# Row tiles issued by GpSimd in one written-out order with the modulation tiles; SyncE issues weight tiles only

## The reference

```python
def first_block(x, c, ...):                  # layers "layer0", "layer1"
    c_act = silu(c)
    for l in range(2):
        sh1, sc1, gt1, sh2, sc2, gt2 = split(c_act @ w_ada[l] + b_ada[l], 6)
        h = x * (1 + sc1) + sh1
        y = token_mixer(h, w_in[l], b_in[l], ...)   # differential, forgetting, retention branches
        x = layernorm(ALPHA * x + gt1 * y, ln_g[l, 0], ln_b[l, 0])
        h = x * (1 + sc2) + sh2
        y = conv_ffn(h, w_up[l], w_conv[l], b_conv[l], w_down[l])
        x = layernorm(ALPHA * x + gt2 * y, ln_g[l, 1], ln_b[l, 1])
    return x

def second_block(x, ...):                    # "middle", then the experts
    x = layernorm(ALPHA_2 * x + gated_deltanet(x, ...), ...)
    x = layernorm(ALPHA_2 * x + swiglu(x, ...), ...)
    x = layernorm(ALPHA_2 * x + swa_sink_attention(x, ...), ...)
    x = layernorm(ALPHA_2 * x + moe_swiglu(x, ...), ...)    # 8 experts, top 2
    return x
```

## Time and profile before

| | |
|---|---|
| median of 3 runs | 2850.41 us (2846.89 to 2853.26) |
| span of the profiled execution | 2847.6 us; its own time outside the profiler is not given |
| PE busy | 2629.9 us, 92% |
| DVE busy | 2177.1 us, 76% |
| ACT busy | 1516.4 us, 53% |
| POOL busy | 24.1 us, 1% |
| DMA | 671.68 MB, mean 236 GB/s |
| chain that ended last | PE 67%, DVE 21%, ACT 5%, issue 4%, DMA 3% |

### The profile page before, as it was taken

One profiled execution on the slowest core, in us unless ns is written; L12 is line 12 of the kernel. 1 busy time (PEld: TensorE's weight loads), 2 busy tenths in 40 slices (PEclk: granted clock), 3 DMA queues, 4 the chain that ended last, 5 costly groups with the idle time before them and its releaser, 6 DMA issues.

```text
span 2847.6 us, 36585 instructions
## 1 busy us (share of the span) xinstructions
PE 2629.9 (92%) x13986; PEld 2234.2 (78%) x13986; DVE 2177.1 (76%) x2738; ACT 1516.4 (53%) x1786; POOL 24.1 (1%) x46
## 2 busy tenths in 40 slices
PE   7889889998998889979989988899999999999997
PEld 6667669876777779868979966788888888888885
DVE  6777677778766777666766556798988989898896
ACT  2344445433344345436334344577777777777774
POOL 0000000000000000000000000000000000000000
PEclk9999999999999999989999999799999999999998
DMA  9743436576544455443125582499999999999994
GB/s 359 273 155 133 143 127 245 200 275 255 213 150 133 144 193 203 163 151 113 45 74 189 173 249 78 189 363 349 370 343 370 343 351 364 347 370 344 368 347 177
DMA packets 104754, 671.68 MB, mean 236 GB/s; under 512 B 11984, under 2 KB 12240, under 8 KB 27136
## 3 DMA queue, kind: packets, MB, share of 16 engines
q1 hardware_dynamic: 97584, 622.08, 59.0%
q0 software_dynamic: 6992, 47.19, 4.9%
HBM read 665.03 MB, written 4.19 MB: 235 GB/s over the span
## 4 chain that ended last, share of the span: by engine, by line
PE 67%; DVE 21%; ACT 5%; issue 4%; DMA 3%; PEld 0%; DVEq 0%; SPq 0%; ACTq 0%; PEldq 0%
PE bank L852 20%; PE bank L854 19%; PE bank L853 19%; DVE W_low L2263 7%; PE bank L1287 3%; ACT W_high L1740 2%; DVE work L2348 1%; DVE arena L2253 1%; DMA arena<-in_w_layer 1%; PE bank L1620 1%; DMA W<-in_w_layer 1%; DMA W<-in_w_middle 1%; DVE work L2580 1%; PE bank L935 1%; DVE acted L2563 1%
## 5 line engine op out<-in xcount | busy, mean ns | idle before, releaser
L2263 DVE TENSOR_TENSOR W_low<-W,W_high 128x1024 fp32r<-128x1024 f32 x426 | 496.7, 1207 | 287.9 <-ACT W_high L1740 282.0
L1740 ACT ACTIVATE W_high<-W 128x1024 fp32r<-128x1024 f32 x426 | 421.8, 1039 | 406.6 <-PE bank L854 186.6
L853 PE MATMUL bank<-W_low,arena_parts 128*128 128x512 f32 (+1 forms) x1128 | 444.8, 394 | 0.0
L852 PE MATMUL bank<-W_high,arena_parts 128*128 128x512 f32 (+1 forms) x984 | 396.5, 403 | 24.3 <-DVE W_low L2263 14.0
L854 PE MATMUL bank<-W_high,arena_parts 128*128 128x512 f32 (+1 forms) x984 | 388.4, 395 | 0.0
L854 PE MATMUL bank<-hT_high,W_low 128*128 128x256 f32 (+2 forms) x1208 | 347.9, 288 | 0.0
L852 PE MATMUL bank<-hT_high,W_high 128*128 128x256 f32 (+1 forms) x1088 | 316.5, 291 | 28.2 <-DVE W_low L2263 20.0
L853 PE MATMUL bank<-hT_low,W_high 128*128 128x256 f32 (+1 forms) x1088 | 311.4, 286 | 0.0
L852 PE MATMUL bank<-W_high,hT_high 128*128 128x512 f32 (+1 forms) x640 | 264.2, 413 | 25.3 <-DVE W_low L2263 11.0
L852 PE MATMUL bank<-arena_parts 128*128 128x512 f32 x672 | 269.4, 401 | 1.5 <-issue 1.5
L853 PE MATMUL bank<-W_low,hT_high 128*128 128x512 f32 (+1 forms) x672 | 266.7, 397 | 0.0
(11 more groups left out here) (428 smaller groups left out, 4791.7 us busy)
## 6 DMA issues: line engine op xcount, KB each, us to landing
W<-in_w_layer SPq DMA_DIRECT2D x170, 1024.0 KB, 4.9
W<-in_w_expert SPq DMA_DIRECT2D x148, 1024.0 KB, 5.1
arena<-in_w_expert SPq DMA_DIRECT2D x114, 1024.0 KB, 4.9
W<-in_w_middle SPq DMA_DIRECT2D x58, 1024.0 KB, 4.9
arena<-in_w_layer POOLq DMA_DIRECT2D x40, 1024.0 KB, 7.3
consts<-in_w_expert SPq DMA_DIRECT2D x37, 1024.0 KB, 4.9
R<-in_w_expert SPq DMA_DIRECT2D x37, 1024.0 KB, 4.9
R<-in_rows_layer SPq DMA_DIRECT2D x70, 256.0 KB, 5.8
```

Of the source, the lines that this page charges most:

```text
L852: mm(bank, lhs[0], rhs[0], start=start, stop=False)
L853: mm(bank, lhs[0], rhs[1], start=False, stop=False)
L1740: do(high_slot(at, w)[:, cols], raw(at, w)[:, cols], ACT.Copy).then_inc(main_highs.filled[main_highs.slot(at, w)], 1)
L2263: tt(lows(at, w)[:, cols], raw(at, w)[:, cols], high_slot(at, w)[:, cols].bitcast(F32), ALU.subtract).then_inc(*low_ready.event(at))
```

## The change

SP's program keeps the weight tiles of the layers and the middle, and loses all 97 row tiles of these parts and the four of the end. POOL's program gets them. For the two layers a list written out by hand, `POOL_LOADS`, puts the row tiles and the modulation tiles into one order; the order within each kind stays as it was. For the middle POOL issues the first eleven row tiles, the two transfers of the bias table with the wait between them, and then the other row tiles, and the four "ln4" rows of the end behind the last expert's slot. Rings, slots, users and the work of PE, DVE and ACT are the same.

```diff
+def _pool_loads(l):
+
+    def ada(*chunks, kind="ada"):
+        return [(kind, c, i) for c in chunks for i in range(2)]
+
+    start = [("A", 0)] + ada(4) if not l else ada(4) + [("A", 0), ("adac", 0)]
+    loads = ([] if l else [("adac", 0)]) + start + [("lam", 0), ("ada", 4), ("A", 1)]
+    loads += ada(5) + [("ada", 5)] if l else [("ada", 5)] + ada(5)
+    loads += [("A", 2), ("B", 0), ("B", 1)] + ada(6) + [("ada", 7, 0), ("B", 2), ("bf", 0), ("C", 0), ("ada", 7, 1)]
+    loads += [("ada", 8, 0), ("C", 1), ("ada", 8, 1), ("C", 2), ("ada", 9, 0), ("ada", 9, 1), ("C", 3), ("C", 4), ("C", 5)]
+    loads += [("gdiff", 0)] + [("gate", c) for c in range(6)] + [("gret", 0), ("gret", 1), ("conv", 0)]
+    loads += [("ln1", r) for r in LN_ROWS] + ada(10) + [("ada", 10), ("ada", 11)]
+    if l + 1 < DEPTH:
+        loads += [("nextc", 0), ("ln2", "g0")] + ada(11) + ada(NEXT[0], kind="next") + [("ln2", "b0")]
+        loads += ada(NEXT[1], kind="next") + [("ln2", "g1"), ("ln2", "b1")]
+        return loads + ada(*NEXT[2:], kind="next")
+    return loads + [("ln2", "g0"), ("ln2", "b0")] + ada(11) + [("ln2", "g1"), ("ln2", "b1")]
+
+
+POOL_LOADS = {p: _pool_loads(l) for l, p in enumerate(LAYERS)}
+for _p in LAYERS:
+    assert [n for n in POOL_LOADS[_p] if n in ADA_LOADS[_p]] == ADA_LOADS[_p]
+    assert [n for n in POOL_LOADS[_p] if n not in ADA_LOADS[_p]] == R_LOADS[_p]
...
-            def load_row(at, name, src):
-                sp.wait_ge(*rows.vacant(at, name))
-                slot = rows.slot(at, name)
-                sp.dma_start(R[:, slot, :], src).then_inc(*rows.fills(at, name))
-
-            def row_source(at, name):
-                n = R_LOADS[at.part].index(name)
-                if name[0] in PER_PARTITION:
-                    n = [r for r in R_LOADS[at.part] if r[0] in PER_PARTITION].index(name)
-                    return ins["cols_" + at.part][n]
-                return ins["rows_" + at.part][n:n + 1, :].to_broadcast([P, 512])
-
-            def load_all(at, after, inputs=None):
+            def load_all(at, inputs=None):
 
                 src = ins["w_" + at.part]
-                done, due = [], []
-
-                def row(name):
-                    load_row(at, name, row_source(at, name))
-                    done.append(name)
-
-                loads = W_LOADS[at.part]
-                for n, name in enumerate(loads):
+                for n, name in enumerate(W_LOADS[at.part]):
                     if name not in ADA_LOADS[at.part]:
                         load_weight(at, name, src[n])
-                        due = [(r, k - 1) for r, k in due]
                     if inputs is not None and name in inputs:
                         inputs[name]()
-                    while due and due[0][1] <= 0:
-                        row(due.pop(0)[0])
-                    if name[:2] in R_LOADS[at.part] and name[:2] + (1 - name[2],) not in loads[n:]:
-                        due.append((name[:2], 2))
-                    due += [(r, 2) for r in after.get(name, [])]
-                for r, _ in due:
-                    row(r)
-                assert done == R_LOADS[at.part], (done, R_LOADS[at.part])
...
-            sp.wait_ge(stream.freed[8], stream.uses(8) + 1)
             at = Pass("end")
-            for name in R_LOADS["end"]:
-                load_row(at, name, row_source(at, name))
...
-            for p in LAYERS:
+
+            def load_row(at, name):
+                n = R_LOADS[at.part].index(name)
+                src = ins["rows_" + at.part][n:n + 1, :].to_broadcast([P, 512])
+                if name[0] in PER_PARTITION:
+                    n = [r for r in R_LOADS[at.part] if r[0] in PER_PARTITION].index(name)
+                    src = ins["cols_" + at.part][n]
+                pool.wait_ge(*rows.vacant(at, name))
+                pool.dma_start(R[:, rows.slot(at, name), :], src).then_inc(*rows.fills(at, name))
+
+            def load_ada(at, name):
+                if name == ("ada", 10, 0):
+                    pool.wait_ge(*group_split.nth(at, 20))
+                pool.wait_ge(*adas.vacant(at, name))
+                n = W_LOADS[at.part].index(name)
+                pool.dma_start(ada_slots[:, adas.slot(at, name), :], ins["w_" + at.part][n]
+                               ).then_inc(*adas.fills(at, name))
+
+            for l, p in enumerate(LAYERS):
                 at = Pass(p)
-                for name in ADA_LOADS[p]:
-                    if name == ("ada", 4, 0) and p == LAYERS[0]:
+                for name in POOL_LOADS[p]:
+                    if name == ("adac", 0) and not l:
+                        pool.wait_ge(*weights.full(at, ("ada", 0, 1)))
+                    if name == ("A", 0) and not l:
                         pool.wait_ge(*weights.full(at, ("A", 0, 0)))
-                    if name == ("ada", 10, 0):
-                        pool.wait_ge(*group_split.nth(at, 20))
-                    pool.wait_ge(*adas.vacant(at, name))
-                    n = W_LOADS[p].index(name)
-                    pool.dma_start(ada_slots[:, adas.slot(at, name), :], ins["w_" + p][n]).then_inc(*adas.fills(at, name))
+                    if name in ADA_LOADS[p]:
+                        load_ada(at, name)
+                    else:
+                        load_row(at, name)
             at = Pass("middle")
+            before_bias = R_LOADS["middle"].index(("bq", 0))
+            for name in R_LOADS["middle"][:before_bias]:
+                load_row(at, name)
             pool.wait_ge(*bias_made.nth(at, 1))
             pool.dma_start(spread, relrow[0:WQ_HEADS, :].unsqueeze(1).to_broadcast([WQ_HEADS, P, 384])
                            ).then_inc(bias_out, 16)
             pool.wait_ge(bias_out, 16)
             shifted = bass.AP(spread.tensor, P - 1, [[383, P], [P * 384, WQ_HEADS], [1, S]])
             pool.dma_start(wbias, shifted).then_inc(bias_in, 16)
+            for name in R_LOADS["middle"][before_bias:]:
+                load_row(at, name)
+            pool.wait_ge(stream.freed[8], stream.uses(8) + 1)
+            for name in R_LOADS["end"]:
+                load_row(Pass("end"), name)
```

More of the change, by code:

```diff
@@ L751, in _ @@
                 at = Pass(LAYERS[l])
-                after = {("out", 0, 1): [("conv", 0)],
-                         ("C", 5, 1): [("gdiff", 0)],
-                         ("gate", 5, 1): [("gret", 0), ("gret", 1)],
-                         ("out", 1, 1): [("ln1", r) for r in LN_ROWS],
-                         ("down", 10, 0): [("ln2", r) for r in LN_ROWS]}
-                if l:
-                    after["A", 0, 1] = [("adac", 0), ("lam", 0)]
-                else:
-                    after["ada", 0, 1], after["A", 0, 1] = [("adac", 0)], [("lam", 0)]
-                if l + 1 < DEPTH:
-                    after["up", 13, 0] = [("nextc", 0)]
-                load_all(at, after, None if l else {("ada", 0, 1): first_inputs, ("A", 1, 1): more_constants})
-            at = Pass("middle")
-            src = W_LOADS["middle"]
-            after = {("ba", 0, 0): [("lnc", 0), ("gconv", 0), ("gpar", 0)],
-                     ("gout", 1, 1): [("ln1", r) for r in LN_ROWS],
-                     ("up", 9, 0): [("relb", 0), ("hot", 0), ("tmask", 0)],
-                     ("down", 10, 0): [("bkv", 0), ("bq", 0), ("ln2", "g0"), ("ln2", "b0")],
-                     ("wq", 0, 1): [("ln2", "g1")],
-                     ("wq", 1, 0): [("ln2", "b1"), ("bq", 1), ("sink", 0)],
-                     ("wob", 1, 0): [("ln3", r) for r in LN_ROWS]}
-            load_all(at, after)
+                load_all(at, None if l else {("ada", 0, 1): first_inputs, ("A", 1, 1): more_constants})
+            at = Pass("middle")
+            load_all(at)
             src = ins["w_expert"]
```

## The result

The changed kernel took 2856.03 us (median of 15 runs, 2852.53 to 2860.59), the kernel before 2849.78 us in the 15 runs beside them (2845.16 to 2857.97). The ratio is 1.0025, 95% interval 1.0017 to 1.0033: slower by 6 to 7 us. Forecast was 2849.1 us, 1.3 us faster, with a range of 2841 to 2856, which the measured median just leaves.

What follows compares the result with a forecast made beforehand. Matmuls on PE were taken as the bound (92% of the span, 67% of the chain). Seven terms, 1.6 + 0.8 + 0.5 - 0.4 - 0.3 - 0.4 - 0.5, gave 1.3 us faster: 2849.1 us, range 2841 to 2856.

Steps and rivals of the forecast that it cites:

- the seven places: Seven places before the experts where a DMA landing is in the chain or just beside it; summed 1.3 us faster.
- the price of company: Delay of a landing by bytes sharing the DMA engines: 2.6 us for 1024 KB, 0.65 for one row tile.
- term 7: Sink, taken by DVE at 1718.28: issued 0.48 us later on POOL, behind a weight tile; loss 0.5, bounds 0 to 1.2.
- End of layer0, gain 1.6: Four ln2 rows leave before weight tile A0, so DVE's wait of 1.71 us goes; bounds 0.8 to 1.7.
- gpar, gain 0.8: Row tile gpar at the middle's start lands with fewer weight tiles beside it; from 2.2 gain to 0.5 loss.
- Block 6 in layer1, gain 0.5: Modulation tile at 687.38 loses two weight tiles beside it, gets two rows ahead; from 2.1 gain to 1.0 loss.
- Block 6 in layer0, loss 0.4: Modulation tile issued at 76.54 gets two rows ahead, with no held weight tile to gain from; loss 0 to 1.0.
- Block 5 in layer0, loss 0.3: Modulation tile at 58.76 gets row ada5 right ahead in its queue; 0 to 0.65 loss, a 0.3 gain possible.
- The exchange in layer1, costed at 0: Modulation tile at 671.48: one row ahead, one weight tile less beside; DVE is busy until it lands, so 0.
- Start, loss 0.4: Column tile adac on POOL runs beside the front weight tile of 14.14 instead of behind it; 0 to 0.65.
- Rival B: Blocks 5, 6 and 7 at each layer's start: rows ahead of modulation tiles push DVE; 6.5 us slower, 2856.9; chance 0.10.
- Rival C: DVE holds up seven POOL issues by 0.49 us each, 3.4 us on top of the forecast: 2852.5; chance 0.08.

Runs made afterwards that it cites:

- piece-by-heads kernel: Changed kernel with five edits of order, plus the bias table sent out in eight pieces of 2 heads and 128 copies, back in four: 2884.97 us, ratio 1.0124.
- the second half: The two layers as in the kernel before, the middle and the end as in the changed kernel: 2852.12 us, ratio 1.0007 to the kernel before.

## Why the prediction was wrong, point by point

The reading of the kernel before held: the wait of 1.7 us at layer0's end went, PE covered the taps, the experts didn't move, and the seven places were nearly the right ones. The sizes failed, and with them the sign of the sum: 1.3 us faster was forecast, and the waits at these places are 5.1 longer.

The step that failed is the price of company: "1024 KB of company thus cost 2.6 us, 256 KB (one row tile) 0.65". It was scaled by bytes from a modulation tile beside a weight tile. Measured at tile (6,0): 4.9 to 5.2 us with no row ahead and the weight tile before it in flight for at most 2.0 us more, 6.8 and 6.9 with one row, 6.7 to 8.6 with two. The first row costs 1.8 us; two cost 3.2 to 3.4 in three of the four landings of the changed kernel, 1.7 in the fourth. At block 6 of the two layers alone the forecast had a gain of 0.1 and the profiles have a loss of 3.8, more than half of the difference. The second failed step is term 7, sink: its landing went to 6.4 us, and the lower clock behind its wait stood in no term.

1. *End of layer0, gain 1.6.* Right: 1.71 and 2.00 to 0.03; in two more kernels with the old order the wait was 0.57 and 1.18, so 1.6 is near the middle of a wide range. The four rows before A0 were the cause, and going earlier on SP's queue does as well.
2. *gpar, gain 0.8.* Nothing came, 7.06 to 7.33 us. gpar was issued at 1267.14, 1.3 us after its release, as worked out, and landed in 6.07 us; lnc, 2.73 us before, took 5.4 beside weight tile qkv4. The term looked at gpar and let lnc go. What was to be had was its slot: lnc had been given the slot that DVE frees last of four.
3. *Block 6 in layer1, gain 0.5.* A loss of 1.3 and 1.7, outside the bound of 1.0. Rows behind the tile: a gain of 1.8 and 1.3.
4. *Block 6 in layer0, loss 0.4.* A loss of 3.1 and 1.5, outside the bound of 1.0. The 0.2 us at the issue was right (0.45 after release); the landing was not.
5. *Block 5 in layer0, loss 0.3.* A gain of 1.0. The tile landed in 8.0 us in place of 9.6; which of its neighbours did it was not tried. The exchange in layer1, costed at 0, was a loss of 1.6 and 0.7.
6. *Start, loss 0.4.* 1.1 (1.4 less the 0.3 at DVE's first wait), bound 0.65.
7. *sink, loss 0.5.* 1.7, bound 1.2, and about 2 more at the lower clock behind it. Sink was issued 0.49 us later as forecast; but it now landed in 6.4 us beside woa1, where it took 4.9 ahead of it.

Rival B (2856.9) came true in the total, in part by luck: at its blocks 5 and 6 it had 6.7 us and the waits have 4.0, and the clock behind sink, which it didn't have, made up for it. Its place at block 6 was right, for a reason next to its own: it priced a row at 1.2 us, which is 0.53 of issue and 0.65 of bytes, and wanted the rows held by their slots; they left as soon as they could and still cost more. Its "decides once the rows move only after the slot of the modulation tile is free" was wrong: B0 was issued a full 1.07 us before the tile. Rival C did not occur: POOL's row issues took 0.54 us at the median and 0.67 at most. The Trainium skill, page "DMA: Bandwidth & Descriptors", section "Issuing engines are not separate DMA queues", says that the transfers of all issuers interleave on the same 16 engines. The traces agree: rows from SyncE slowed GpSimd's tile as well (6.2 us in layer0, where it took 4.9 to 5.2 without them). That the rule alone had given 2852.0, nearer than the forecast, is luck: it struck out term 1, which came.

Left open: why a row of 256 KB costs 1.8 us, where 1024 KB of a weight tile cost 2.6; one shared line, the issuing queue and the weight tile behind were each tried and none is it alone. In layer1 of the piece-by-heads kernel (6,0) took 7.8 us with no row ahead, where B(1,0) was in flight for 3.5 us more; in the kernel before it took 7.2 and 6.7 us beside one in flight for 4.6 and 3.6 us more. So the price of a row can't be told from one landing, and it is no constant.

## What to carry to other kernels

Price a transfer ahead of an awaited one from a landing with and without it, not by its share of the bytes; here that was nearly three times too little. A wait in a queue is no cost by itself and freeing it no gain: releasing small transfers early moves them in front of the large one that is waited for, so put what is needed next first, and everything that has time behind it. Give the first user of a stage the slot of the ring that is freed first. When a new wait stands in front of TensorE's work, look at the granted clock behind it as well: here it cost about 2.6 us behind a wait of 1.8.

## What the runs showed that was not expected

- Cutting a transfer is not neutral: 384 KB from two partitions landed in 21.4 us at the median, with DMA at 0.67; the same bytes from 16 partitions in 7.4 us, at 0.90. The first slows every tile beside it.
- After a pause PE stayed at the lower clock for 3.0 us in one run and 6.2 in another over the same work, 1.4 us later for it. Behind a wait of 1.8 us for sink the clock was 0.79 and 0.83 where it was 0.89 and 0.94 without the wait. Together such places made 4.0 of the 10.8 us between the first two profiles. Runs of one kernel lie up to 17 us apart (2840.64 to 2857.92, the second half), so that places of 1 to 3 us are read from waits, not from medians.
